# Layer 0 and 1: two conditioning pairs behind the layer norm, and the weights' loads issued on ScalarE's queue

## What is computed

```
cond = silu(c)
mod = cond @ w_ada[l] + b_ada[l]            # 2048 -> 6 * 2048
sh1, sc1, g1, sh2, sc2, g2 = split(mod, 6)
u = x * (1 + sc1) + sh1
y = even_mixer(u) if l == 0 else odd_mixer(u)
x = layer_norm(ALPHA * x + (1 + g1) * y, ln_g[l, 0], ln_b[l, 0])
u = x * (1 + sc2) + sh2
y = (gelu(causal_conv(g)) * a) @ w_down[l]  where a, g = split(u @ w_up[l])
x = layer_norm(ALPHA * x + (1 + g2) * y, ln_g[l, 1], ln_b[l, 1])
```

## Time and profile before

| what | us |
|---|---|
| median of 3 runs | 2451.17 |
| lowest and highest | 2449.59, 2452.19 |
| the profiled execution, its own time | 2450.96 |
| its span in the profile | 2449.1 |
| PE busy | 2264.4 |
| DVE busy | 1677.7 |
| ACT busy | 1005.7 |

### The profile page before, as it was taken

One profiled execution on the slowest core, in us unless ns is written; L12 is line 12 of the kernel. 1 busy time (PEld: TensorE's weight loads), 2 busy tenths in 40 slices (PEclk: granted clock), 3 DMA queues, 4 the chain that ended last, 5 costly groups with the idle time before them and its releaser, 6 DMA issues.

```text
span 2449.1 us, 25903 instructions
## 1 busy us (share of the span) xinstructions
PE 2264.4 (92%) x10251; PEld 1865.1 (76%) x10251; DVE 1677.7 (69%) x1586; ACT 1005.7 (41%) x1004; POOL 8.5 (0%) x19
## 2 busy tenths in 40 slices
PE   4779998699999999999988999998999999999996
PEld 3567767588877788887767888876888788888885
DVE  6678989686768676758756676776867555555455
ACT  2334432344433344443343445434444334444432
POOL 1000000000000000000000000000000000000000
PEclk9889998799999999999989999998999999999998
DMA  9998979487769787758838777774877556555553
GB/s 317 320 373 321 349 251 345 177 302 242 273 225 324 254 281 248 272 182 300 323 127 320 253 257 263 269 271 150 293 248 273 165 186 209 182 189 189 164 189 128
DMA packets 392218, 612.52 MB, mean 250 GB/s; under 512 B 21113, under 2 KB 205073, under 8 KB 390562
## 3 DMA queue, kind: packets, MB, share of 16 engines
q1 hardware_dynamic: 391442, 610.52, 72.1%
q0 software_dynamic: 448, 0.25, 0.0%
q10 hardware_dynamic: 208, 0.10, 0.0%
HBM read 608.70 MB, written 2.10 MB: 249 GB/s over the span
## 4 chain that ended last, share of the span: by engine, by line
PE 77%; DVE 10%; DMA 5%; issue 4%; ACT 3%; SPq 0%; DVEq 0%; ACTq 0%
PE bank L1123 24%; PE bank L1125 24%; PE bank L1132 23%; DMA ada_w<-in_w_ada 5%; DVE ada_acc L740 3%; DVE w_lo L730 2%; PE bank L1145 2%; DVE ada_acc_alt L740 2%; PE bank L1179 2%; ACT w_hi L483 1%; DMA w_raw<-in_w_qkv 1%; DVE x_tok L797 1%; PE bank L1142 1%; DVE y_gated L793 1%; ACT u_f L632 1%
## 5 line engine op out<-in xcount | busy, mean ns | idle before, releaser
L730 DVE TENSOR_TENSOR w_lo<-w_raw,w_hi 128x2048 fp32r<-128x2048 f32 x380 | 848.1, 2233 | 486.3 <-ACT w_hi L483 425.6
L483 ACT ACTIVATE w_hi<-w_raw 128x2048 fp32r<-128x2048 f32 x380 | 709.8, 1870 | 1035.2 <-PE bank L1125 732.3
L1123 PE MATMUL bank<-w_hi,u_hi 128*128 128x512 f32 (+1 forms) x2176 | 869.4, 401 | 20.3 <-DVE u_lo L781 14.7
L1125 PE MATMUL bank<-w_hi,u_lo 128*128 128x512 f32 (+1 forms) x2176 | 851.5, 392 | 0.0
L1132 PE MATMUL bank<-w_lo,u_hi 128*128 128x512 f32 (+1 forms) x2176 | 531.9, 387 | 7.9 <-DVE w_lo L730 7.9
L1123 PEld LDWEIGHTS bank<-w_hi,u_hi 128*128 128x128 f32 x2176 | 418.2, 192 | 112.4 <-issue 20.6
L1125 PEld LDWEIGHTS bank<-w_hi,u_lo 128*128 128x128 f32 x2176 | 417.6, 192 | 86.4 <-issue 3.8
L1132 PEld LDWEIGHTS bank<-w_lo,u_hi 128*128 128x128 f32 x2176 | 405.3, 188 | 91.3 <-DVE w_lo L730 8.6
L740 DVE SCALAR_TENSOR_TENSOR ada_acc<-ada_w,silu_c,ada_acc 128x1024 f32<-128x1024 f32 x285 | 364.9, 1280 | 32.7 <-DMA ada_w<-in_w_ada 22.3
L1123 PE MATMUL bank<-w_hi,hid_hi 128*128 128x512 f32 x688 | 276.0, 401 | 0.0
L1125 PE MATMUL bank<-w_hi,hid_lo 128*128 128x512 f32 x688 | 274.4, 399 | 0.0
(11 more groups left out here) (178 smaller groups left out, 1122.3 us busy)
## 6 DMA issues: line engine op xcount, KB each, us to landing
ada_w<-in_w_ada SPq DMA_DIRECT2D x384, 512.0 KB, 6.4
w_raw<-in_w_up SPq DMA_DIRECT2D x344, 512.0 KB, 4.7
w_raw<-in_w_down SPq DMA_DIRECT2D x152, 512.0 KB, 4.8
w_raw<-in_w_qkv SPq DMA_DIRECT2D x96, 512.0 KB, 4.8
w_raw<-in_w_in_ab SPq DMA_DIRECT2D x64, 512.0 KB, 7.5
w_raw<-in_w_out_ab SPq DMA_DIRECT2D x32, 512.0 KB, 6.6
w_raw<-in_w_o SPq DMA_DIRECT2D x32, 512.0 KB, 4.9
w_raw<-in_w_down SPq DMA_DIRECT2D x40, 256.0 KB, 3.3
```

Of the source, the lines that this page charges most:

```text
L483: nc.scalar.activation(whi[:, u % HL_SLOTS, 0:width], raw[:, u % RAW_SLOTS, 0:width], ACT.Copy).then_inc(w_hi, 1)
L730: nc.vector.tensor_tensor(wlo[:, u % HL_SLOTS, 0:width], raw[:, u % RAW_SLOTS, 0:width], whi[:, u % HL_SLOTS, 0:width].bitcast(f32), ALU.s ...
L1123: nc.tensor.matmul(banks[t][:, 0:width], h_at(kt, t), w, start=first and n == 0, stop=False)
L1125: ins = nc.tensor.matmul(banks[t][:, 0:width], l_at(kt, t), w, start=False, stop=False)
```

## The change

- The last two of layer 0's four MLP shift and scale pairs (8, 9) move from units 36 to 45 to units 45 to 54, behind the layer norm; pairs 20 and 21 of layer 1 from 214 to 238 to units 243 to 252. The rows of the others are spread anew, pairs 12 to 15 one row per unit. Sums stand two units behind the last row (one for pairs 8, 9, 20, 21, which are summed into a transposition bank).
- `UP_ORDER`: the first three chunks of up_a run with interleaved quarters, (0,0) (1,0) (0,1) (1,1) (2,0) (2,1), then the late quarters of all three. Pieces 4 to 7 are transposed early and parked in `x_norm_T`; ACT applies scale and shift once their quarter of mod is there (`ln_park`, `ln_late_piece`, `ln_quarters`). `QKV_FIRST`: the first two chunks of qkv are interleaved in the same way; pieces 2 to 7 are transposed between its first units.
- Unit loads leave SP: `load_unit` is on ACT's queue, behind `hi_unit`, with the same two DMAs per unit. SP keeps rows, gates and tables.
- Pairs 0 to 3 use eight row slots instead of four; some small tables move in memory or later or earlier by a few units.

```diff
-RAW_SLOTS, HL_SLOTS, ADA_SLOTS = 4, 2, 4
+RAW_SLOTS, HL_SLOTS, ADA_SLOTS, ADA_FIRST = 4, 2, 4, 8
...
+UP_ORDER = [(0, 0), (1, 0), (0, 1), (1, 1), (2, 0), (2, 1)] + [(c, j) for j in (2, 3) for c in (0, 1, 2)]
+QKV_FIRST = [(c, j) for j in range(4) for c in (0, 1)]
...
-    fill(4, 15, [3, 3, 3, 3, 3, 3, 3, 4, 3, 3, 3, 4, 3, 4, 3])
-    fill(7, 30, [2, 1, 2, 2, 3, 5, 4, 4, 4, 2, 4, 2, 4, 2, 4, 3])
...
+    fill(4, 15, [2, 2, 3, 2, 2, 3, 2, 2, 3, 2, 2, 3, 2, 2, 2, 1, 1, 1, 1, 2, 4, 4, 3, 3, 1, 3, 1, 3, 1, 1])
+    for layer, m in ((0, 8), (1, 20)):
+        first = PH[layer, "up_a"]["unit"]
+        fill(m, first - 3, [2, 2, 0, 3, 3, 3, 3])
+        fill(m + 1, first + 4, [5, 5, 6])
+        fill(m + 2, first + 16, [1, 2, 1] * 4)
+        fill(m + 3, first + 28, [1, 2, 1] * 4)
+    first = PH[0, "down_a"]["unit"] + 3
+    for m in range(12, 16):
+        fill(m, first + KT * (m - 12), [1] * KT)
+    fill(16, first + 64, [1, 1, 1, 2, 1, 1, 1, 1, 1, 2, 1, 1, 1, 1])
+    fill(17, first + 78, [1, 2, 1] * 4)
     first = PH[1, "qkv"]["unit"]
+    fill(18, first + 4, [1] * KT)
+    fill(19, first + 23, [1] * KT)
...
+    sum_at = {m: s + 2 for m, s in ends.items()}
+    sum_at |= {m: ends[m] + 1 for m in (8, 9, 20, 21)} | {1: 2, 2: 12, 3: 16, 6: 39}
...
         @block.scalar
         def _(act):
+            def load_unit(u):
+                if u < N_UNITS:
+                    act.wait_ge(w_lo, u + 1)
+                    for dst, src in unit_halves(u):
+                        act.dma_start(dst, src).then_inc(w_loaded[u % RAW_SLOTS], 16)
...
                 nc.scalar.activation(whi[:, u % HL_SLOTS, 0:width], raw[:, u % RAW_SLOTS, 0:width], ACT.Copy
                                      ).then_inc(w_hi, 1)
+                if u >= HL_SLOTS:
+                    load_unit(u + RAW_SLOTS - HL_SLOTS)
...
+            act.wait_ge(a_step, A0 + 11)
+            for u in range(RAW_SLOTS):
+                load_unit(u)
...
+            def ln_late_piece(s, v):
+                act.wait_ge(sem("ln_quarter"), s + v // 2 - 1)
...
+            def up_first(layer):
+                for e in range(len(UP_ORDER)):
+                    if e in (1, 5, 8):
+                        for v in {1: (2, 3), 5: (4, 5), 8: (6, 7)}[e]:
+                            ln_lo(s, v)
+                    lo_unit(PH[key]["unit"] + e + 2)
+                    beside(PH[key]["unit"] + e)
```

More of the change, by code:

```diff
@@ L353, in load_unit @@
                         load_row(m, r)
[L355 to L382, removed]
-                                 w[:, k0 + a:k0 + b, c, :]) for a, b in ((0, half), (half, k))])
             def gate_load(layer, part, uses):
@@ L466, in _ @@
             mlp(1, 16)
+            sp.wait_ge(a_sum, SUM_NO[23, 1] + 1)
             ln_load(3)
@@ new lines, in up_first @@
+            def up_first(layer):
+                key, s = (layer, "up_a"), 2 * layer
+                out_h = hid_out(key)
+                for v in range(2):
+                    ln_piece(s, v)
+                for e in range(len(UP_ORDER)):
+                    hi_unit(PH[key]["unit"] + e + 2)
+                    if e == 0:
+                        ln_piece(s, 2)
+                        ln_piece(s, 3)
+                    if e in (1, 2):
+                        ln_park(s, 2 * e + 2)
+                        ln_park(s, 2 * e + 3)
+                    if e in (4, 7):
+                        for v in (4, 5) if e == 4 else (6, 7):
+                            ln_late_piece(s, v)
+                    if e == 9:
+                        out_h(0)
+                    if e == 10:
+                        hidden(layer, "up_a", 0)
+                    if e == 11:
+                        out_h(1)
@@ L774, in steps @@
                             mid(c)
-                        if norm is not None and c == lo:
-                            ln_affine(norm, j - 2)
+                        if key[1] == "up_a" and c == 4 and j in (3, 4):
+                            ln_affine(2 * key[0], j - 1)
                         beside(unit_no(key, c, j - 2))
@@ L900, in mlp @@
                     prev = lambda c: hidden(layer, name, c - 1)
-                    steps(key, 0, 1, norm=2 * layer if name == "up_a" else None)
-                    steps(key, 1, 11 if name == "up_b" else last + 1, mid=prev)
+                    if name == "up_a":
+                        up_first(layer)
+                    else:
+                        steps(key, 0, 1)
+                    steps(key, 1 if name == "up_b" else 4, 11 if name == "up_b" else last + 1, mid=prev)
                     if name == "up_b":
@@ L1181, in hidden_T, with up_first, mlp @@
                 ins.then_inc(h_T, 1)
-            def mlp(layer, u_from):
+            def up_first(layer):
+                key, s = (layer, "up_a"), 2 * layer
+                ph, late_pair = PH[key], UP_PAIRS[layer][1]
+                ln_T(s, (0, 1))
+                for e, (c, j) in enumerate(UP_ORDER):
+                    u = ph["unit"] + e
+                    if j == 0:
+                        pe.wait_ge(acc_free, ph["chunk"] + min(c, 1) + 1)
+                    if c == 2 and j == 0:
+                        pe.wait_ge(a_out, SUM_NO[UP_PAIRS[layer][0], 0] + 1)
+                    unit(u, [(k, 4 * j + k) for k in range(4)], (uhi, ulo), j == 0, j == 3,
+                         bank[UP_BANKS[c]:UP_BANKS[c] + 2], 2 + U_LN[s] + 2 * j + 2)
+                    if e < 3:
+                        ln_T(s, (2 * e + 2, 2 * e + 3))
+                    if e == 4:
+                        pe.wait_ge(t_free, 2 + T_LN[s] + 8)
+                    if e == 10:
+                        pe.wait_ge(a_out, SUM_NO[late_pair, 0] + 2)
+                        hidden_T(layer, "up_a", 0)
+                    beside(u)
+            def mlp(layer):
                 for name in ("up_a", "up_b"):
```

332 lines of the change are left out of this document (205 added, 127 removed).

## The result

The changed kernel takes **2408.48 us** (median of 4 runs, 2407.5 to 2410.94) against 2451.22 us for the kernel before (2449.59 to 2452.19): a ratio of 0.9828, 95% interval 0.9811 to 0.9845, or 42.7 us gained. The prediction was 2389.0 with a range of 2362 to 2425. The sign and the range held; a third of the forecast gain is missing. Runs are compared by their medians, stages by the profiled execution of each.

The account below looks back on a forecast made before the run. PE, busy 92%, mostly runs at its matmul floor after layer 0's front, where conditioning rows (DMA and DVE) set the pace. Terms -55 + 40 - 16.5 - 14 + 1 - 6 - 9 + 1 - 3.5 = -62 gave 2389 us, range 2362 to 2425.

Parts of the forecast that it names:

- The queue move itself: cost 0: All 380 units: issuing loads from ACT, 0.98 us per unit, 370 us in all, was to cost nothing.
- the freed SP is worth part of the -55: Before unit 48: unit loads no longer behind SP's row waits were to give part of the front's 55 us gain.
- w_hi waiting for DMA w_raw rarely: Sign to look for in the profile: high parts of units seldom wait for their unit's load to land.
- The front: Start to unit 48: fewer, spread rows and fewer holes save 55 us, bounds 36 and 75; unit 48 near 413.
- The burst: Deferred rows beside the first units of up_a: +20 us per layer, +40 in all, bounds +10 and +35.
- T+73: Unit 57's start after unit 48's start T, counted by DVE alone; T+77 with the four slots, 57.0 us before.
- The bound of +35: Upper bound per layer on the burst: all 28 rows at four slots' round trip, 8.2 us per four.
- Attention's start: Pair 18's first row still waits 15 us behind table and gate; interleaved first eight units alone give -3.5 us.
- Rival 1: Up_a's first units: four slots pace a heavier burst, +35 us per layer, 2419 us; chance 0.16.
- Rival 2: Bandwidth stays the pace and the queue does nothing: front -36, attention 0, 2411 us; chance 0.14.
- Rival 3: Up_a's first units: light burst, DVE's lag swallowed, +10 us per layer, 2369 us; chance 0.14.
- Rival 4: ACT's issue lands on PE, slower: break-even 0.16 us per unit, 2484 us at 0.25; chance 0.06.

Follow-up runs that it names:

- run 1: Changed kernel with the unit loads back on SyncE's queue, ahead of the same unit's rows: 2389.02 us, ratio 0.9744.
- run 3: Changed kernel with ScalarE issuing each load ahead of the waits of that unit's high part instead of behind it: 2401.08 us, ratio 0.9789.
- run 4: run 3 with the two u pieces made ahead of the high parts of units 0 and 1: 2396.35 us, ratio 0.977.
- run 5: run 1 with two small DMAs per unit issued on ScalarE's queue where the change has its loads: 2396.48 us, ratio 0.977.
- run 2: Kernel before with only the unit loads moved to ScalarE's queue, nothing of the plan: 2478.09 us, ratio 1.011.
- run 7: Changed kernel with rows of pairs 8 and 9 loaded in 256 of 1024 columns, VectorE's work whole: 2398.26 us in a single execution.
- run 9: run 1 and run 8 together, with the bias table and gate row issued three units later: 2361.47 us, ratio 0.9628.
- run 8: Changed kernel with layer 1's pairs 20 and 21 back in attention, layer 0 still deferred: 2382.45 us, ratio 0.9723.
- run 10: run 9 with pair 8 back in the front and only pair 9 deferred in layer 0: 2349.44 us, ratio 0.9579.

## Why the prediction was right, and where its sum failed

**The failed step is "The queue move itself: cost 0", with "the freed SP is worth part of the -55".** It was worth none of it: with the loads on SyncE behind the rows, unit 48 starts at 411.3 (run 1), with them on ScalarE at 421.0. The move costs 19.5 us in the changed kernel and 26 alone. The step priced the issue rightly (370 us in all, 374 measured) and counted on a load having 9 us before ScalarE wants it; "w_hi waiting for DMA w_raw rarely" became 25 waits and 89.3 us, where the kernel before had 3 and 20.9. It did not ask what stands *before* the issue on ScalarE, though it had a rival about what stands behind it. Of the 19.5 us:

- 7.4 us were the load's place behind the waits of the high part (run 3), with the reserve named there. ScalarE waits for PE and VectorE; SyncE, in the kernel before, waited mostly for slots. Ahead of unit 37 the DMA engines are busy 0.56 of the time, at 155 GB/s; then the late loads and the rows fall together and the engines are full while VectorE waits for rows (windows of the changed kernel):

```profile
321.00:326.00 5.00, 5.00 (x23) 4.13 (x22) 4.69 (x9) 3.65 (x6) 0.00 (x0) 1.00 0.56 155
...
336.00:341.00 5.00, 0.57 (x6) 0.33 (x4) 3.07 (x3) 0.00 (x0) 0.00 (x0) 0.84 1.05 408
```

- 4.7 us were the order at the start (run 4). The changed kernel makes the high parts of units 0 and 1 ahead of the u pieces, the kernel before behind them; the prediction has no term for it.
- 7.3 us are left between run 4 and run 1, mostly in layer 0's burst (units 48 to 57, 4.7 us) and behind both bursts (58 to 72 and 256 to 286, 1.6 each). ScalarE's issue time (at most 7.5 by run 5) or the units' loads going ahead of the rows: which of the two stays open. For the second speak, a little, VectorE's waits for rows of pair 9 between units 48 and 57, first in run 1, then in run 4:

```profile
DVE ada_acc_alt L827 <- DMA ada_w<-in_w_ada: 2.8, 3, 2.1
```

```profile
DVE ada_acc_alt L829 <- DMA ada_w<-in_w_ada: 4.2, 6, 1.2
```

The Trainium skill (DMA: Bandwidth & Descriptors, Queues, rings and completion order) says that each DMA engine takes turns between the queues it has work for, packet by packet. A row on SyncE's ring would then share with a unit's load instead of going in the order SyncE chose. The row of run 2 that took 18.1 us while loads issued behind it landed first, and these waits, agree with that; no run isolates it in the changed kernel. The same page's rule that the prediction cited, that a second issuing engine saves issue time only, was right that there is no bandwidth to gain and said nothing of a loss.

**The other terms**, changed kernel / without the queue move / predicted, where the first two are stages of the traces against the kernel before:

| term | changed | run 1 | predicted |
|---|---|---|---|
| front, to unit 48 | -47.0 | -56.7 | -55 |
| bursts, layers 0 and 1 | +24.5, +26.0 | +21.2, +21.2 | +20, +20 |
| down_a of layer 0 | -15.8 | -15.8 | -16.5 |
| down_b with layer norm | -16.4 | -16.3 | -14 |
| attention's start, units 182 to 192 | +1.4 | -1.1 | -3.5 |
| attention | -8.6 | -8.6 | -9 |
| end of up_a, layers 0 and 1 | -2.8, -2.7 | -2.7, -2.8 | -3, -3 |
| sums in layer 1's down_a | +1.8 | +1.8 | +1 |

The column of run 1 adds up to -59.8 of a difference in spans of -60.1, against a forecast of -62 with up_b's +1. Every term is within 2.4 us of the forecast, but the front hides larger misses that cancel.

- **The front.** Run 1 has unit 48 at 411.3 for a forecast of 413, with one queue, so the gain over VectorE's 36 us did not need the loads taken away from behind SyncE's 6.26 us stalls. It did not come from the 28 fewer rows either. The plan fills pairs 1 to 3, the rows up to unit 14, as before, and the stages to unit 3, 10 and 16 still give 3.3, 10.8 and 9.4 us (forecast 4, 7 and 8), 23.5 in all. Behind unit 16, where the 28 rows go, run 1 gains 33.2 (forecast 36). What gives the 23.5 is the eight slots, the later sums or the tables that moved; they were not separated. Nor is the spread behind unit 15 as even as the forecast has it: 4, 4, 3 and 3 rows stand beside units 35 to 38, where the hole of unit 37 is.
- **The burst.** The mechanism came as written: a hole of 2.86 us (forecast 4) before the unit that needs u_lo 4 and 5, a sum of pair 9 that waits for its last rows. The count by VectorE alone gave T+73 and run 7 measures 76.0; 1.7 of the 3 us missed are the clock, since the sum behind the hole takes 3.57 us and not the 1.92 of the other at 455.99. The four slots were put at 4 us; the rows' DMA costs 5.5 in the changed kernel (81.5 against 76.0), but 3.3 of them go with the queue move, since run 1 takes 78.2. Of the 4.5 and 6.0 us over the forecast of 20 the queue move's are 3.3 and 4.8; without it both bursts are 1.2 over. The bound of +35 does not follow from its working: seven times 8.2 us is 57.4, as long as the stage was before, and what comes on top is not given.
- **Attention's start.** That the row keeps its 15 us behind table and gate was right (16.4 now). The -3.5 for the interleaved units was not: with the hole behind unit 189 unchanged the earlier end of the pieces only moved time into it. Run 9 gets 8.4 us by moving the table.

**The rivals.** Rival 1, a heavier burst (+35 per layer, 2419), falls: 24.5 and 26. Rival 2 named 2411, within 3 us of the result, and is still false: its front of -36 is -47. A right time for a wrong reason, which only the stages tell. Rival 3's light burst falls with +10. Rival 4 had the right engine and the wrong size: 19.5 us over 380 units is 0.05 us each, against its break-even of 0.16. Its mechanism, work standing behind the issue, is at most 7.5 us of it (run 5); the other 12 are the order (runs 3 and 4). That PE would not wait for w_hi throughout held. Unit 48 at 421 lies between the 413 foreseen and the 430 at which the prediction called itself wrong.

## What to carry to other kernels

When a DMA moves to another engine's queue, list what that engine waits for ahead of the issue, not only what its issue delays: a load belongs before the waits of the work it stands beside, and at a start behind nothing that the first matmul needs. A second queue gave no bandwidth where one already kept the DMA engines at a share near 1, and it took away the order between rows and loads that one queue had. Deferring work pays only where the stage it leaves was bound by it: in layer 1 deferring both pairs lost 26 us (run 8), in layer 0 one pair beat two by 12 us (run 10), and whether one beats none was not run.

## What the runs showed of the hardware

- Eight half-megabyte DMAs issued in a row took ScalarE 9.34 us, and not evenly: the first five 0.47 to 0.49 each, the last three 1.60, 2.49 and 2.60, about the 2.7 us between two of their landings. Two in a row take 0.90 to 0.94, about SyncE's 0.98. The price of one issue depends on how many went out just before it.
- Splitting the traffic over two queues changed most median landing times little: rows 6.2 us against 6.5 in run 1, units of up 5.0 against 4.7, of in_ab 7.2 against 8.0, but units of out_ab 6.7 against 5.1. The medians hide single late ones, such as the 18.1 us of run 2.
- The 16 small matmuls of a conditioning sum take 1.9 us at 456.0, at a granted clock of 1.00 (2.4 GHz), and 3.6 us at 491.0, at 0.50 (1.2 GHz), behind a hole of 10.2 us: such a hole is paid a second time at the lower clock. The length of the last hole alone does not tell the clock: the hole before the first sum is 2.18 us, and in run 9 the same sum behind 2.16 us took 3.54 us at 0.50.
